# A two-branch recurrent decoder layer on one core: an output stage that reads its input early and takes squares at eviction, and inverse rounds that stay on one half of the array

## What is computed

```python
h = rms_norm(x, norm_pre)
z = h @ w_in                                   # 2048 -> 18640 columns
oa = rwkv7(z ...)                              # 32 heads of 64, matrix state per head
ob = gla(z ...)                                # 4 heads, gated linear attention
m = sigmoid(ga) * oa + sigmoid(gb) * ob
o = m @ w_out                                  # 2048 x 2048
y = x + o * rsqrt(mean(o * o) + eps) * norm_post
```

## Time and profile before

| | |
|---|---|
| median of 3 runs | 3253.73 us (3245.68 to 3255.68) |
| the profiled execution | 3255.16 us, span in the profile 3253.6 us |
| PE busy | 3017.0 us (93%) |
| DVE, ACT, POOL busy | 1736.9, 1057.7, 400.3 us |
| granted TensorE clock, mean | 0.967 of full speed |
| head-pair stage, one turn | about 120 us |
| output stage, from its first DMA issue to the end | 2976.5 to 3253.6 us |

### The profile page before, as it was taken

The page is one execution under the profiler, slowest core; times in us unless marked ns, Lnnn a source line. Parts: engine busy times, 40 slices in busy tenths (PEclk is TensorE's granted clock), DMA queues, the critical chain, the costliest instruction groups (busy, mean ns, idle before and its releaser), DMA issues. The chain is left out here.

```text
span 3253.6 us, 79535 instructions
## 1 busy us (share of the span) xinstructions
PE 3017.0 (93%) x33815; PEld 2771.8 (85%) x33815; DVE 1736.9 (53%) x2561; ACT 1057.7 (33%) x1686; POOL 400.3 (12%) x804
## 2 busy tenths in 40 slices
PE   4899999999997899999999999999999999994995
PEld 3898897997985898899899899899899899893995
DVE  3264454444544564665565565565566565464224
ACT  4332332331431243243243243243243243242222
POOL 2200101001003121021021021021022022011000
PEclk7999999999998999999999999999999999996998
DMA  3323423324324222232132132132122122223322
GB/s 94 98 66 89 154 65 122 108 66 130 99 59 130 57 74 56 61 81 63 47 81 67 42 81 68 42 81 69 50 73 68 46 76 68 54 55 135 88 77 97
DMA packets 368528, 255.11 MB, mean 78 GB/s; under 512 B 19412, under 2 KB 347600, under 8 KB 366288
## 3 DMA queue, kind: packets, MB, share of 16 engines
q1 hardware_dynamic: 342592, 184.18, 20.7%
q0 software_dynamic: 25600, 66.02, 6.5%
HBM read 212.69 MB, written 37.45 MB: 77 GB/s over the span
## 5 line engine op out<-in xcount | busy, mean ns | idle before, releaser
L203 PE MATMUL psum<-act_hi,w_hi 128*128 128x280 f32 (+2 forms) x5184 | 1591.1, 307 | 59.0 <-DVE w_lo L189 41.2
L205 PE MATMUL psum<-act_hi,w_lo 128*128 128x280 f32 (+2 forms) x5184 | 1519.7, 293 | 0.4 <-issue 0.4
L204 PE MATMUL psum<-act_lo,w_hi 128*128 128x280 f32 (+2 forms) x5184 | 1518.2, 293 | 0.0
L203 PEld LDWEIGHTS psum<-act_hi,w_hi 128*128 128x128 f32 (+1 forms) x5184 | 984.8, 190 | 133.6 <-issue 93.7
L204 PEld LDWEIGHTS psum<-act_lo,w_hi 128*128 128x128 f32 (+1 forms) x5184 | 984.7, 190 | 4.5 <-issue 1.0
L205 PEld LDWEIGHTS psum<-act_hi,w_lo 128*128 128x128 f32 (+1 forms) x5184 | 984.6, 190 | 0.6 <-issue 0.6
L189 DVE TENSOR_TENSOR w_lo<-raw,w_hi 128x1024 fp32r<-128x1024 f32 (+1 forms) x324 | 396.2, 1223 | 243.7 <-ACT w_hi L181 231.6
L181 ACT CAST w_hi<-raw 128x1024 fp32r<-128x1024 f32 (+1 forms) x324 | 339.3, 1047 | 41.8 <-DMA raw<-in_w_in_dram 15.0
L1619 POOL DMA_DIRECT2D out_s_rwkv_dram<-arena x128 | 77.7, 615 | 1436.2 <-ACT arena L1758 1436.2
L2061 PE MATMUL psum<-arena 64*64 64x64 f32 x9984 | 210.2, 225 | 45.6 <-DVE arena L1880 27.2
L2061 PEld LDWEIGHTS psum<-arena 64*64 64x64 f32 x9984 | 185.2, 135 | 74.9 <-issue 74.6
(11 more groups left out here) (330 smaller groups left out, 3364.7 us busy)
## 6 DMA issues: line engine op xcount, KB each, us to landing
raw<-in_w_in_dram SPq DMA_DIRECT2D x288, 512.0 KB, 4.4
arena<-in_state_gla_dram POOLq DMA_DIRECT2D x32, 512.0 KB, 5.1
out_s_gla_dram<-arena POOLq DMA_DIRECT2D x32, 512.0 KB, 3.3
raw<-in_w_out_dram SPq DMA_DIRECT2D x32, 512.0 KB, 4.4
ob_dram<-arena POOLq DMA_DIRECT2D x16, 280.0 KB, 3.2
arena<-ob_dram POOLq DMA_DIRECT2D x16, 280.0 KB, 4.8
m_dram<-arena POOLq DMA_DIRECT2D x16, 280.0 KB, 2.6
arena<-m_dram SPq DMA_DIRECT2D x4, 1120.0 KB, 12.0
```

The source lines that it names most:

```text
L203: pe.matmul(out, hi, act_hi[:, k, cols], start=(k == 0), stop=False)
L204: pe.matmul(out, hi, act_lo[:, k, cols], start=False, stop=False)
L205: mm = pe.matmul(out, lo, act_hi[:, k, cols], start=False, stop=(k == KT - 1))
```

## The change

**Inverse rounds.** In rounds 0 to 3 chunks 0 to 3 stay on the halves on which `t_d` and `n_d` lie: the operand half is the result half. The products with the identity go, so do the separate start of `inv` for chunks 0 to 3 and the copy after each round: one addition over all nine chunks takes their place each time. `DV` is the count of DVE instructions in a turn: six fewer.

```diff
-DV, DS, DG = 55, 11, 5
+DV, DS, DG = 49, 11, 5
...
-                    for h in range(2):
-                        tt(inv[64 * h:64 * h + 64, 0:CROSSED], gram[0:64, 0:CROSSED, h, 0:C], bc(block16[0:64], CROSSED), MUL).then_inc(mine.sem, 1)
-                        dve.wait_ge(mine.sem, mine.next(i))
-                    tt(inv[:, 0:CROSSED], inv[:, 0:CROSSED], bc(eye2, CROSSED), ADD).then_inc(mine.sem, 1)
-                    dve.wait_ge(mine.sem, mine.next(i))
-                    tt(inv[:, CROSSED:NC], n_d[:, CROSSED:NC], bc(eye2, NC - CROSSED), ADD).then_inc(inv_ready.sem, 1)
+                    tt(inv, n_d, bc(eye2, NC), ADD).then_inc(inv_ready.sem, 1)
...
                         if n > 0:
-                            dve.tensor_copy(inv[:, 0:CROSSED], pair(2, 0, CROSSED).rearrange("p (c t) -> p c t", c=CROSSED)).then_inc(mine.sem, 1)
-                            dve.wait_ge(mine.sem, mine.next(i))
-                            tt(inv[:, CROSSED:NC], inv[:, CROSSED:NC], pair(2, CROSSED, NC - CROSSED).rearrange("p (c t) -> p c t", c=NC - CROSSED),
-                               ADD).then_inc(inv_b.sem, 1)
-                            dve.wait_ge(inv_b.sem, inv_b.next(i))
+                            both(lambda c, b: tt(inv[:, c, :], inv[:, c, :], b(2), ADD), inv_b)
...
-                    each(6, of(t_d), of(n_d), crossed=(1, 0))
+                    each(6, of(t_d), of(n_d))
...
-                    each(6, of(t2), of(x2), crossed=(0, 1))
-                    each(4, of(x2), of(t2), crossed=(0, 1))
-                    each(2, of(t2), of(inv), inv_mm, crossed=(0, 1), keep=True)
+                    each(6, of(t2), of(x2))
+                    each(4, of(x2), of(t2))
+                    each(2, of(t2), of(inv), inv_mm)
```

```diff
+                sp.wait_ge(pd.half.sem, pd.half.at(LAST_TURN, 12))
+                sp.wait_ge(stored.sem, stored.at(LAST_TURN, 0))
+                sp.dma_start(act_lo[:, 0:LAST_TURN, :].bitcast(F32), m_dram[0:LAST_TURN].rearrange("j p t -> p j t")).then_inc(load_m[0].sem, 16)
...
-                for n in range(4):
-                    sp.dma_start(m_in[:, 4 * n:4 * n + 4, :], m_dram[4 * n:4 * n + 4].rearrange("j p t -> p j t")).then_inc(load_m[n].sem, 16)
+                sp.dma_start(act_lo[:, LAST_TURN:NPAIR, :].bitcast(F32), m_dram[LAST_TURN:NPAIR].rearrange("j p t -> p j t")).then_inc(load_m[1].sem, 16)
...
-                    nc.scalar.copy(act_hi[:, j, :], m_in[:, j, :]).then_inc(m_hi.sem, 1)
+                    nc.scalar.copy(act_hi[:, j, :], act_lo[:, j, :].bitcast(F32)).then_inc(m_hi.sem, 1)
                     act.wait_ge(m_hi.sem, m_hi.next(i))
+                    if j == 3:
+                        pe_.split_hi(act, 0, a_order, 0)
...
+                            if i == t == 0 and step < KT:
+                                pe.wait_ge(m_lo.sem, step + 1)
```

```diff
+                def squares_of(i, t, part):
+                    act.wait_ge(o_taken.sem, o_taken.at(i, 2 * t + part + 1))
+                    for n, tok in enumerate(((0, 1), (2, 3, 4))[part]):
+                        w = P if tok < 4 else 32
+                        signal = a_order if n < 1 + part else o_squared
+                        nc.scalar.activation(o_t[2][0:w, 0:P], bank[4 + 2 * part][0:w, n * P:(n + 1) * P], ACT.Square,
+                                             accum_out=squares[0:w, tok, 2 * i + t:2 * i + t + 1]).then_inc(signal.sem, 1)
+                        act.wait_ge(signal.sem, signal.next(i))
...
+                    pe_.split_hi(act, i, a_order, 1)
+                    evacuate(i, 0, 0)
+                    squares_of(i, 0, 0)
+                    evacuate(i, 0, 1)
+                    if not last:
+                        pe_.split_hi(act, i, a_order, 2)
+                    squares_of(i, 0, 1)
+                    evacuate(i, 1, 0)
+                    squares_of(i, 1, 0)
+                    evacuate(i, 1, 1)
+                    squares_of(i, 1, 1)
...
-                            dve.tensor_copy(o_rows[:, tt_, col], bank[b][:, 0:2 * P].rearrange("p (a c) -> p a c", a=2)).then_inc(signal.sem, 1)
+                            dve.tensor_tensor(o_rows[:, tt_, col], bank[b][:, 0:2 * P].rearrange("p (a c) -> p a c", a=2),
+                                              bc(norm_row[:, col], 2), MUL).then_inc(signal.sem, 1)
...
+                dve.tensor_reduce(sums, squares, mybir.AxisListType.X, ADD).then_inc(summed.sem, 1)
...
-                    dve.scalar_tensor_tensor(out=o, in0=o, scalar=stats[0:n, 10 + t:11 + t], in1=norm_row[0:n, :], op0=MUL, op1=MUL).then_inc(mine.sem, 1)
-                    dve.tensor_tensor(o, o, x_rows[t % 3][0:n, :], ADD).then_inc(y_rows.sem, 1)
+                    dve.scalar_tensor_tensor(out=o, in0=o, scalar=sums[0:n, t:t + 1], in1=x_rows[t % 4][0:n, :], op0=MUL, op1=ADD).then_inc(y_rows.sem, 1)
...
-                    if t >= 3:
-                        pool.wait_ge(y_rows.sem, t - 2)
+                    if t == 4:
+                        pool.wait_ge(y_rows.sem, 1)
...
-                    pool.dma_start(x_rows[t % 3][0:n, :], src).then_inc(load_x[t].sem, 16)
+                    pool.dma_start(x_rows[t % 4][0:n, :], src).then_inc(load_x[t].sem, 16)
```

More of the change, by code:

```diff
@@ L1435, in build @@
         masks = sig("d_masks")
+        load_m = [sig(f"e_load_m{n}") for n in range(2)]
         def save(eng, i, mine, t):
@@ L2052, in half_of, with each @@
                         return head[1 - h if crossed and c < CROSSED else h]
-                    def each(b, left, right, signal=None, crossed=(1, 1), keep=False):
+                    def each(b, left, right, signal=None, crossed=(1, 1)):
                         for c in CHUNK_ORDER:
[L2057 to L2062, removed]
+                            for h in range(2):
+                                out = pair(b, c, 1)[half_of(c, h, crossed[1])]
+                                at = half_of(c, h, crossed[0])
+                                m = mm(out, left(c)[at], right(c)[at], start=True, stop=True)
                         if signal:
@@ L2116, in turn_of @@
                     pe.sem_inc(waited.sem, 1)
-                    each(4, of(n_d), of(t_d), inv_mm, crossed=(1, 0))
+                    each(4, of(n_d), of(t_d), inv_mm)
                     run(3)
@@ L2137, in turn_of @@
                     pe.sem_inc(waited.sem, 1)
-                    each(2, of(x2), of(inv), inv_mm, crossed=(0, 1), keep=True)
+                    each(2, of(x2), of(inv), inv_mm)
                     run(3)
@@ L2251, in build @@
         o_rows = ar(5, D)
[L2252 to L2255, removed]
+        x_rows = [ar(D) for _ in range(4)]
         norm_row = ar(D)
-        o_t = [ar(TOK) for _ in range(2)]
+        o_t = [ar(TOK) for _ in range(2)] + [ar(P)]
         shift_rows = x_rows[2][0:48, 0:9 * P]
         lora_rows = ar(LORA)
-        stats = ar(16)
+        squares, sums = ar(5, NPAIR), ar(5)
         pe_ = Projection("e", 2)
@@ L2332, in _ @@
                     act.wait_ge(m_hi.sem, m_hi.next(i))
-                act.sem_inc(pe_.half.sem, 3)
-                pe_.split_hi(act, 0, a_order, 0)
-                def turn(i, last=False):
-                    mine = a_order
-                    for t in range(2):
-                        if not (last and t):
-                            pe_.split_hi(act, i, mine, t + 1)
-                        for half in range(2):
-                            act.wait_ge(pe_.half.sem, pe_.half.at(i, 2 * t + half + 1))
-                            if half == 0:
-                                act.wait_ge(o_turned.sem, o_turned.at(i, 2 * t - 2))
-                            nc.scalar.copy(o_t[t][:, half * TOK // 2:(half + 1) * TOK // 2], bank[half][:, 0:TOK // 2]).then_inc(pe_.evacuated.sem, 1)
-                            act.wait_ge(pe_.evacuated.sem, pe_.evacuated.next(i))
@@ L2362, in _ @@
+                for i in range(TURNS):
+                    if i:
+                        again(pe_.evacuated, o_squared, a_order)
+                    turn(i, last=i == TURNS - 1)
+                mine, i = s_order, 0
+                act.wait_ge(summed.sem, summed.at(i, 1))
+                nc.scalar.activation(sums, sums, ACT.Sqrt, scale=1.0 / D, bias=tiny[:, 0:1]).then_inc(rooted.sem, 1)
+                act.wait_ge(rooted.sem, rooted.next(i))
             @block.vector
@@ L2417, in _ @@
                 pe.sem_inc(o_taken.sem, 2)
-                pe.wait_ge(m_lo.sem, NPAIR)
-                with pe.Fori(0, TURNS) as i:
+                pe.sem_inc(o_squared.sem, 2)
+                for i in range(TURNS):
                     def turn(t, part):
@@ L2424, in turn @@
                         pe.wait_ge(o_taken.sem, o_taken.at(i, 2 * t + part - 1))
+                        pe.sem_inc(waited.sem, 1)
+                        pe.wait_ge(o_squared.sem, o_squared.at(i, 2 * t + part - 1))
                         pe.sem_inc(waited.sem, 1)
@@ L2430, in _ @@
                     for t in range(2):
```

(6 more changed lines are left out.)

67 lines of the change are left out of this document (35 added, 32 removed).

## The result

The changed kernel takes 3216.35 us, median of 4 runs (3214.82 to 3217.28); the kernel before took 3250.61 us in the runs beside it (4, from 3245.68 to 3255.68). The ratio is 0.9899 [0.9885, 0.9914]: 34 us less, where 15 were forecast.

What follows compares the result with a forecast made beforehand. PE was taken to bound the head-pair and output turns, with gaps at the stage change and the end. +15.8 - 18.8 - 12.1 + 0.5 = -14.6 us from a 3253.7 us median gave 3239 us, range 3223 to 3254.

Steps and rivals of the forecast that it cites:

- Part 1: Inverse rounds, head-pair stage: uncrossed products cost 28.8 ns each, +0.99 us a turn, +15.8 us over 16 turns.
- Rival 2: Inverse rounds: products on one way hold those behind them, 43 ns an instruction, +80 us, 3303 us; chance 0.06.
- Rival 1: Inverse rounds cost PE nothing, so +15.8 us falls out: 3223 us, or 3189 at full crossed rate; chance 0.12.
- Part 2: Output stage start, from T0 (SP's first issue there): m loaded early, -18.8 us, between -21 and -16.
- Part 3: End of the kernel, first square to last addition: 26.95 us becomes 14.4, less store lag, -12.1 us.
- Part 4: Output turns: new squares on ACT and written-out loops cost little, +0.5 us taken for instruction stops.
- The second tile is not late: Output stage start: second tile's weights cast at about T0 + 19, needed by PE at T0 + 26.
- Rival 3: Output stage start gains little, m late or slow clock holding: 6 us for 18.8, 3252 us; chance 0.13.
- rival 4: Written-out output turns stall PE over 1 us a turn, 8 to 10 us in all, 3248 us; chance 0.08.

Runs made afterwards that it cites:

- e8: The kernel before with only the four hardware loops of the output stage written out; ratio to the kernel before 1.0001.
- e6: The changed kernel with DVE's three old instructions that start `inv` put back, their results unused; ratio to the kernel before 0.9977.
- e9: The kernel before with the change's output stage, DVE's small addition moved ahead of the weight subtraction, and prompt loads of `x` delayed; 3187.33 us, ratio 0.9811.

## Why the prediction was right in direction and wrong in size

- **Part 1, the price of an instruction, right.** 1.26, 3.36 and 2.31 us for 36, 108 and 72 instructions, 29 ns each, and a shortest turn that grew by 0.94 us instead of 0.99. Rival 2's price, 43 ns, is refuted by these groups. Rival 1 has the time, 3223 for 3216, but not the mechanism: the rounds do cost PE what I said.
- **Part 1, the sum, wrong, and this is the step that failed.** "All 16 turns have these rounds: +15.8 us" multiplied the difference of one almost undisturbed turn, turn 14 (0.7 us above the shortest). Measured were -6.2 us in 15 turns and -0.8 us in the last: 22.8 us beside the forecast and of the other sign, so that the direction of the whole came out by parts 2 and 3. The 15 turns give 15 x 0.94 = +14.1 and the excess 4.7 - 25.0 = -20.3. The excess was in my rows: "issue: 13.9, 26 stops" stands on the line of these very products. I used it to price the code of part 4, and did not ask at which of the products PE stopped, nor what the new pace does to it: these are waits for instructions, most of which the slower rounds take away, and with the wait for DVE the dips go too. The dips I had not looked for: the stage's mean clock is shown as 1.00.
- **Part 2, mis-sized by 5.1 us.** -13.7 for -18.8. The first half ended at T0 + 21.5, close to the T0 + 19 to 21 of the text; the second half lost the rest, to the late weights (PE stood still for 3.17 us) and the slow clock behind the wait (some 1.5 us). "The second tile is not late" was wrong: I had compared when its weights are cast with when PE needs them, but not counted the loads of `x` that share the DMA engines, nor the eviction queued behind the cast on ACT. Rival 3's 6 us was too little.
- **Part 3, right.** -11.3 for -12.1; the stores of 1 MB land in 5.7 us at the new pace, as far as I had allowed for.
- **Part 4, right.** -0.6 us for +0.5, e8 shows nothing for the loops, and rival 4 did not come.
- **The base.** The profiled execution of before had a stretch of half clock that the one of after has not, 7.8 us in the table; the medians, 34 us apart, are the fairer measure. The other five lines of the table sum to 32.6 us, so by them the miss is the 22.8 us of part 1, less the 5.1 of part 2, and small ones.

## What to carry to other kernels

Before the change of one stretch is multiplied by the number of turns, compare all turns with the shortest: if they are longer in sum, find where, because a change of pace can remove that too. Set a stop of PE that the profile calls "issue" beside the packets of the instruction queue: where it ends just behind one, PE waited for instructions, and the stop goes or stays with the pace of the products around it. A wait of PE costs more than its length when the clock falls behind it: here one small addition, moved ahead of a large instruction on DVE, took out the wait and nearly all dips, 29 us, and with that the crossed rounds are the faster ones again.

## What was not expected of the hardware

- PE stopped for up to 2.4 us inside a run of small products at 16.6 ns each; at 29 ns, or with projection matmuls between them, the stops inside were some 0.7 us at most.
- All 46 stops of PE of more than 0.6 us without a releaser, in 15 turns of each of the fourteen kernels, ended 1.2 to 1.6 us after a packet of 16 KB on the instruction queue, whatever their length.
- The granted clock fell from 1.00 to 0.50 for some 3.4 us behind single standstills of some 1.7 us or more in an otherwise busy engine (5 to 7 times in 15 turns), and not behind the waits of 1.3 us in e6; once, in e9, behind a stop of 0.74 us.
- A weight load of 512 KB took 15.3 us beside loads of 1 MB (4.8 us when these were held back), and 22.3 us behind one of 4.2 MB, for 4.6 us in the median.
